# Fifteen halo tiles of h transposed by DMA from SP in place of TensorE: a hybrid attention and pooling layer on eight cores

## The chip, the cores and the metric

The kernel runs as one program on the 8 cores of one Trainium2 chip. Each core computes 1,024 of the 8,192 tokens (batch 2, sequence 4,096) and nothing is exchanged between cores: what a core needs of earlier tokens it computes again from its own copy of x. The metric is the device time in microseconds (us) of the slowest core.

Engines by their names in the profile: PE (TensorE matmul) and PEld (its weight load), DVE (VectorE), ACT (ScalarE), POOL (GpSimd), SP (SyncE). SPq, ACTq and POOLq are the same engines issuing DMAs.

## The reference

```python
for _layer in range(DEPTH):                       # DEPTH = 1, x is (2, 4096, 2048)
    h = rms_norm(x, norm_gain)
    proj = jnp.einsum('bsd,de->bse', h, w_in)     # 16384 columns: q, k, v, z_attn, u_pool, z_pool, gates
    ...
    # --- mixer A: 3 groups (window, dilation) = (128,1), (512,4), (2048,16), 8 heads of 128 each
    q = rms_norm(q.reshape(shp), q_norm_gain)
    k = rms_norm(k.reshape(shp), k_norm_gain)
    for g, (window, dilation) in enumerate(DILATED_GROUPS):
        o_g, lse_g = dilated_window_attention(partial_rope(q[:, :, g], pos), partial_rope(k[:, :, g], pos),
                                              v[:, :, g], window, dilation)
    ...
    y_attn = jnp.einsum('bsc,cd->bsd', attn * jax.nn.silu(z_attn), w_branch_attn)
    # --- mixer B: mean over the last 2, 4, 8, 16 tokens minus the token, a 256x256 map per group
    y_pool = jnp.einsum('bsc,cd->bsd', pool * jax.nn.silu(z_pool), w_branch_pool)
    merged = g_attn * y_attn + g_pool * y_pool
    x = x + jnp.einsum('bsd,de->bse', merged, w_out)
```

A query attends to keys up to 2,048 tokens back. A core therefore needs h of its own 1,024 tokens and of the 2,048 tokens ahead of them, the halo, of which k and v are taken.

## The kernel before, in words

**Stages.** (1) The norm and transpose of 24 tiles of x (128 tokens by 2,048 channels each), and beside it the pooling branch: the projections u (`u_block`, `u_group`) and z (`zp_block`, `z_early`) with the pooling and its maps (`u_pool`, `pool_map`). (2) Twelve rounds of attention: `proj_v` for two heads, then `proj_qk` and `attention` for each. (3) Gates, merge and the output projection.

**The tiles of x.** `tiles` orders them: own tiles 0 to 8 as j = 0 to 8 (tile 8 holds 16 own tokens and 112 of the halo), then the halo tiles 14, 13, 12, 0, 1, ..., 11 as j = 9 to 23. For each, `x_task(j)` makes this sequence: ACT squares the tile of x with a sum (L538, writes `xn` as scratch) and takes Ln and Exp of the sum (L462); DVE multiplies (L473) and writes the normed tile `xn`; SP issues the load of tile j+3 into the buffer of `xt` that is now read; PE transposes `xn` in 16 blocks of 128x128 into two banks `p_pnd` (L557), 8 blocks each; ACT (first half of a halo tile, L466) and DVE (second half, L574) copy these to `hTh` (halo) or `hTo` (own), the transposed h that all projections read. `xt` has 3 buffers, `xn` has 2, so that the square of tile j writes the buffer that tile j-2 used. The halo tiles' parts carry `heavy=XLATE`: they are taken up only while the planner sees ACT and DVE less than 4 us behind PE.

**What sets the order.** `Sched.op` appends each instruction to the list of its engine and derives its waits from the buffers that it reads and writes; it also keeps planned times, with a cost for each instruction. `Tasks.pump` and `need_tiles` put pieces of the live tasks between the projection's matmuls by those planned times. Each engine then runs its list in order. A DMA's planned cost is 0.1 us on its engine, and its end comes from `kb` over 540 KB per us and 2.2 us of latency; the real one plays no part in the order.

**The hand-over to stage 2.** The tensors of stage 2 (`vSb`, `vSc`, `kS`, `qS`, `E`, `ND`, `rot`) lie in the memory of `xt`, `xn`, `gb`, `ua`, `ub` and `pt`. `inherit(b, p1)` makes the first write to each of them wait for every user of all of those. The first such write is ACT's copy of `proj_v` from a `p_pp` bank to `vSb` (L466). `p_pp` has 3 banks.

**SP's list in stage 1** holds the loads of x (L513) and the spills `pt_spill<-s_pt` of the pooling branch (L682), which are read back in stage 3. In stage 2 it holds the small copies `s_rot<-s_kS` and `s_rot<-s_qS` within SBUF (L848, L850; 16 partitions each). Weights are loaded from POOL (L481).

Of the kernel before, what the change touches and what calls it, by code (L numbers as in the profile page):

```python
# [11 lines left out]
KC = 16  # L12
# [292 lines left out]
def build_program(debug=False):  # L305
# [16 lines left out]
    with es:  # L322
# [4 lines left out]
        def place(name, shape, dt, at=None):  # L327
            n = 1
            for s in shape[1:]:
                n *= s  # L330
            nbytes = n * (4 if dt == F32 else 2)
            if at is None:
                at = pos[0]
                pos[0] += ((nbytes + 31) // 32) * 32
                assert pos[0] <= limit, (name, pos[0], limit)
            assert at + nbytes <= limit, (name, at, nbytes, limit)
            return nc.alloc_sbuf_tensor_at("s_" + name, shape, dt, offset=at)
# [18 lines left out]
        hTh = place("hTh", [128, KC, THALO], BF16)  # L356
# [21 lines left out]
        xn_t = [zA.put(f"xn{i}", [128, D], BF16) for i in range(2)]  # L378
# [40 lines left out]
        def psb(name):  # L419
# [5 lines left out]
        pnd_t = [psb(f"pnd{i}") for i in range(2)]  # L425

        semnames = (["pe", "act", "dve", "pool", "sp"] + [f"dw{i}" for i in range(NW)]
                    + [f"dx{i}" for i in range(4)] + [f"dc{i}" for i in range(8)] + [f"dp{i}" for i in range(3)]
                    + [f"drot{i}" for i in range(4)] + [f"dwo{i}" for i in range(4)]
                    + [f"dr{i}" for i in range(4)] + [f"do{i}" for i in range(4)])  # L430
        sems = {k: es.enter_context(nc.semaphore("s_" + k)) for k in semnames}
        S = Sched(nc, sems)
# [3 lines left out]
        B_hH = [Buf(f"hH{i}") for i in range(16)]  # L436
# [28 lines left out]
        def acopy(out, in_, n, reads, writes):  # L465
            S.op("act", lambda a: a.copy(out=out, in_=in_), reads=reads, writes=writes, cost=0.17 + n * 0.00083)  # L466
# [30 lines left out]
        xn = Ring(xn_t, "xn")  # L497
# [3 lines left out]
        def issue_x(j):  # L501
            wh, ti = tiles[j]
            i = xt.take("x")
            loaded[j] = i
            if wh == "o" and ti == 8:
                inherit(B_x8, [xt.B[i]])
                S.op("sp", lambda s: s.dma_start(out=xt_t[i][0:16, :], in_=xh[NTOK - 16:NTOK, :]),
                     writes=[xt.B[i]], dsem=f"dx{i}", kb=128)
                S.op("sp", lambda s: s.dma_start(out=xt_t[i][16:128, :], in_=xh[THALO - 128:THALO - 16, :]),
                     writes=[B_x8], dsem="dx3", kb=896)  # L510
                return
            row = ti * 128 if wh == "h" else THALO - PRE + ti * 128
            S.op("sp", lambda s: s.dma_start(out=xt_t[i][:], in_=xh[row:row + 128, :]),  # L513
                 writes=[xt.B[i]], dsem=f"dx{i}", kb=1024)
# [12 lines left out]
        def x_task(j):  # L527
            wh, ti = tiles[j]
            own = wh == "o"
            x8 = [B_x8] if own and ti == 8 else []  # L530

            def gen(me):
                yield Cond(after=[tile_front[j - 1]] if j else [])
                xi = loaded[j]
                c0 = 3 * j
                yield Cond(reads=[xt.B[xi]] + x8, rings=[xn], heavy=0.0 if own else XLATE)
                ni = xn.take(me)
                S.op("act", lambda a: a.activation(out=xn_t[ni][:], in_=xt_t[xi][:], func=AF.Square,  # L538
                                                   accum_out=stat[:, c0:c0 + 1]),
                     reads=[xt.B[xi], B_stat0] + x8, writes=[xn.B[ni], B_st[j]], cost=2.1)  # L540
                act(stat[:, c0 + 1:c0 + 2], stat[:, c0:c0 + 1], AF.Ln, 1, [B_st[j]], [B_st[j]], bias=float(D * EPS))
                act(stat[:, c0 + 2:c0 + 3], stat[:, c0 + 1:c0 + 2], AF.Exp, 1, [B_st[j]], [B_st[j]], scale=-0.5,
                    bias=float(0.5 * np.log(D)))
                stt(xn_t[ni][:], xt_t[xi][:], stat[:, c0 + 2:c0 + 3], gb[:], ALU.mult, ALU.mult, 2048,
                    [xt.B[xi], B_st[j], B_gb] + x8, [xn.B[ni]], cost=2.35)
                xt.free(xi)
                tile_front[j].done = True
                if j + 3 < 24:
                    if x8:
                        inherit(xt.B[xi], x8)  # L550
                    issue_x(j + 3)
                for half in range(2):
                    yield Cond(reads=[xn.B[ni], B_id], rings=[pnd], heavy=0.0 if own else XLATE)
                    pi = pnd.take(me)
                    for k8 in range(8):
                        kc = half * 8 + k8
                        S.op("pe", lambda t, kc=kc, k8=k8, pi=pi: t.transpose(  # L557
                            tp_t[pi][:, k8 * 128:(k8 + 1) * 128], xn_t[ni][:, kc * 128:(kc + 1) * 128], ident[:]),
                            reads=[xn.B[ni], B_id], writes=[pnd.B[pi]], cost=0.056)
                    ks = slice(half * 8, half * 8 + 8)  # L560
                    i_ap = tp_t[pi].rearrange("p (k c) -> p k c", c=128)
                    if not own:
                        parts = [(hTh[:, ks, ti * 128:ti * 128 + 128], i_ap, 1024, B_hH[ti])]
                    elif ti < 8:
                        parts = [(hTo[:, ks, ti * 128:ti * 128 + 128], i_ap, 1024, B_hO[ti])]
                    else:
                        parts = [(hTo[:, ks, TOWN:TOWN + PRE], i_ap[:, :, 0:16], 128, B_hO[8]),
                                 (hTh[:, ks, THALO - 128:THALO - 16], i_ap[:, :, 16:128], 896, B_hH[15])]
                    on_act = half == 0 and (not own or ti % 2 == 1)
                    for (o_ap, p_ap, n, bd) in parts:  # L570
                        if on_act:
                            acopy(o_ap, p_ap, n, [pnd.B[pi]], [bd])
                        else:
                            S.op("dve", lambda v, o_ap=o_ap, p_ap=p_ap: v.tensor_copy(out=o_ap, in_=p_ap),  # L574
                                 reads=[pnd.B[pi]], writes=[bd], cost=0.1 + n * 0.00058)
                    pnd.free(pi)
                xn.free(ni)
                if own and ti == 0:
                    acopy(hTh[:, :, THALO - PRE:THALO], hTo[:, :, 0:PRE], 256, [B_hO[0]], [B_hH[15]])
            return gen  # L580
# [154 lines left out]
        for j in range(9):  # L735
# [6 lines left out]
            if j == 5 or j == 6:  # L742
                z_early(j - 5, w01[2 + j - 5], 0)
        S.op("pool", lambda g: g.dma_start(out=pm[:], in_=pmaps.rearrange("p (g e) -> p g e", g=8)),
             writes=[B_pm], dsem="dc3", kb=1024)
# [373 lines left out]
        for b in [B_pT, B_wo[1]] + tga.B + tgp.B:  # L1119
            inherit(b, B_hH)  # L1120
        S.op("sp", lambda s: s.dma_start(out=pT[:], in_=pt_d.rearrange("p (e t) -> p e t", e=8)),
             reads=[B_ptd], writes=[B_pT], dsem="dp1", kb=2048)
        S.op("dve", lambda v: v.tensor_scalar_mul(out=halfb[:], in0=cst[:, C_BG:C_BG + 32], scalar1=0.5),
             reads=[B_cst], writes=[B_halfb])
# [62 lines left out]
        for cg in range(4):  # L1187
            cs = slice(512 * cg, 512 * cg + 512)
            for tt_ in range(8):
# [4 lines left out]
                    out=xr_t[xi][:], in_=xh[THALO + 128 * tt_:THALO + 128 * tt_ + 128, cs]),  # L1194
                    writes=[xr.B[xi]], dsem=f"dr{xi}", kb=256)
                P, BP = banks[n_out % 4]
                n_out += 1
                for db in range(KC):
# [5 lines left out]
                     reads=[ob.B[oi]], dsem=f"do{oi}", kb=256)  # L1204
# [90 lines left out]
```

How the kernel before makes its waits and increments, by code:

```python
        def run(ename, eng):  # L144
            w = waited[ename]
            for o in streams[ename]:
                for k, d in o.deps.items():
                    if d.eng == "pe" and ename == "pe" and not d.isdma:
                        continue
                    if w[k] < d.semval:
                        eng.wait_ge(sems[k], d.semval)
                        w[k] = d.semval
                ins = o.fn(eng)
                if o.signal:
                    ins.then_inc(sems[o.key], 16 if o.isdma else 1)
            for k, v in final.items():
                if w[k] < v:
                    eng.wait_ge(sems[k], v)
                    w[k] = v
```

## Time and profile before

| | us |
|---|---|
| median of 3 runs | 1662.37 |
| lowest and highest of the 3 | 1601.19 and 1837.11 |
| the profiled execution | 1614.29 |
| its span (core 5, the slowest; the others 1588.8 to 1611.1) | 1612.7 |
| PE busy in it | 1561.1 (97%) |
| DVE, ACT, POOL busy | 635.7, 607.3, 86.9 |
| stage 1 to the first copy to `vSb` | 0 to 224.8 |

The span runs from the first to the last instruction of a core; 1.6 us of the profiled execution lie around it. A busy share is an average over all stages; what a change of stage 1 is worth has to be read in stage 1.

### The profile page before, as it was taken

The page shows a single profiled execution, that of the slowest core. Times are in us where ns is not written, and L with a number is a line of the kernel's source. Part 1 is how long each engine was busy: PE and PEld are TensorE (multiplying, and loading weights), DVE is VectorE, ACT ScalarE, POOL GpSimd, SP SyncE. Part 2 cuts the span into 40 slices and gives each one's busy share as a digit, 9 for nine tenths or more (in the row PEclk, how much of TensorE's full clock was granted, in tenths as well). Part 3 has the DMA queues.
Part 4 walks back from the last instruction along what each step waited for, and adds up shares of the span by engine and source line. Part 5 has one row for each costly group of instructions (what it writes and reads, how often), then busy time and mean ns, then how long its engine had stood idle before and what let it go on. Part 6 is the DMA issues. An engine that isn't in the chain of part 4 may idle for free.

```text
span 1612.7 us, 26994 instructions; the slowest of 8 cores (1588.8 to 1612.7 us)
## 1 busy us (share of the span) xinstructions
PE 1561.1 (97%) x10192; PEld 939.6 (58%) x10192; DVE 635.7 (39%) x830; ACT 607.3 (38%) x988; POOL 86.9 (5%) x168
## 2 busy tenths in 40 slices
PE   4699999999999999999999999999999999999998
PEld 4455575946694567667847784757444444444443
DVE  4676714136433636445056523535531111112221
ACT  4655525344434544545354434553641111111000
POOL 0000000000000000000000000000001100000000
PEclk9988879999999999999999999999999999999999
DMA  8997334031403233333113222133535566542895
GB/s 240 228 229 170 86 59 85 4 58 35 84 3 66 52 53 56 67 58 57 27 34 67 54 40 47 34 71 59 126 70 85 104 105 104 92 72 47 181 215 126
DMA packets 43071, 139.08 MB, mean 86 GB/s; under 512 B 7040, under 2 KB 8064, under 8 KB 39552
## 3 DMA queue, kind: packets, MB, share of 16 engines
q0 software_dynamic: 23552, 85.58, 31.4%
q1 hardware_dynamic: 14640, 43.33, 8.7%
q10 hardware_dynamic: 4752, 8.44, 2.6%
q8 instruction: 83, 1.36, 0.3%
q14 instruction: 44, 0.36, 0.1%
HBM read 207.90 MB, written 10.49 MB: 135 GB/s over the span
## 4 chain that ended last, share of the span: by engine, by line
PE 93%; DMA 2%; ACT 2%; DVE 1%; issue 1%; ACTq 0%; DVEq 0%; SPq 0%; POOLq 0%
PE p_pp L458 77%; PE p_pnd L458 6%; PE p_psc L458 5%; PE p_pS L458 4%; PE p_pnd L557 1%; DMA s_xt<-xh 1%; ACT s_xn L538 1%; DMA pt_spill<-s_pt 1%; DMA s_wr<-w_in 1%; DVE s_xn L473 1%; ACT s_rr L462 1%; DVE s_rr L469 0%; ACT s_stat L462 0%; ACT L538 0%; DVE s_hTo L574 0%
## 5 line engine op out<-in xcount | busy, mean ns | idle before, releaser
L458 PE MATMUL p_pp<-s_hTo,s_wr 128*128 128x512 bf16 (+4 forms) x3616 | 781.2, 371 | 14.6 <-DVE s_hTo L574 6.8
L458 PEld LDWEIGHTS p_pp<-s_hTo,s_wr 128*128 128x128 bf16 x3616 | 347.5, 100 | 384.1 <-issue 47.9
L473 DVE SCALAR_TENSOR_TENSOR s_kS<-p_pp,s_cst,s_rr 128x512 bf16<-128x512 f32 (+1 forms) x96 | 94.7, 986 | 282.2 <-ACT s_rr L462 279.2
L458 PE MATMUL p_pp<-s_wr,s_hTo 128*128 128x256 bf16 x1536 | 178.7, 276 | 0.0
L458 PEld LDWEIGHTS p_pp<-s_wr,s_hTo 128*128 128x128 bf16 x1536 | 161.6, 119 | 8.9
L458 PE MATMUL p_pp<-s_wr,s_hTh 128*128 128x256 bf16 x1344 | 162.0, 275 | 2.3 <-ACT s_vSb L466 2.3
L458 PE MATMUL p_pp<-s_hTh,s_wr 128*128 128x512 bf16 (+1 forms) x768 | 155.3, 353 | 0.0
L462 ACT ACTIVATE s_rr<-p_pS 128x512 f32<-128x512 f32 x144 | 83.6, 581 | 181.2 <-PE p_pS L458 175.2
L458 PEld LDWEIGHTS p_pp<-s_wr,s_hTh 128*128 128x128 bf16 x1344 | 145.9, 137 | 6.3 <-issue 2.9
L462 ACT ACTIVATE s_rr<-s_rr 128x512 f32<-128x512 f32 x208 | 128.6, 618 | 19.2 <-ACT s_rr L462 0.4
L481 POOL DMA_DIRECT2D s_wr<-w_in x128 | 67.6, 529 | 1265.9 <-PE p_pp L458 806.3
L458 PEld LDWEIGHTS p_pp<-s_hTh,s_wr 128*128 128x128 bf16 x768 | 70.5, 98 | 75.5 <-issue 0.6
L462 ACT ACTIVATE s_sq<-p_pp 128x512 bf16<-128x512 f32 x144 | 83.1, 577 | 55.3 <-PE p_pp L458 55.2
L473 DVE SCALAR_TENSOR_TENSOR s_tga<-s_tga,p_psc 128x512 f32<-128x512 f32 x32 | 22.0, 687 | 206.6 <-PE p_psc L458 206.6
L462 ACT ACTIVATE s_tga<-p_pp,s_halfb 128x512 f32<-128x512 f32 x32 | 22.0, 687 | 166.7 <-PE p_pp L458 166.6
L458 PE MATMUL p_pp<-s_wo,s_mT 128*128 128x512 bf16 x384 | 84.2, 379 | 0.0
L462 ACT ACTIVATE s_E<-p_psc 128x512 bf16<-128x512 f32 x96 | 57.5, 599 | 59.2 <-PE p_psc L458 58.4
L473 DVE SCALAR_TENSOR_TENSOR s_xn<-s_xt,s_stat,s_gb 128x2048 bf16<-128x2048 f32 x24 | 56.4, 2351 | 45.2 <-ACT s_stat L462 44.7
L473 DVE SCALAR_TENSOR_TENSOR s_qS<-p_pp,s_cst,s_rr 128x512 bf16<-128x512 f32 x48 | 48.5, 1011 | 61.9 <-ACT s_rr L462 58.1
L469 DVE TENSOR_TENSOR s_E<-s_E,s_mskb 128x512 bf16<-128x512 bf16 x96 | 40.8, 425 | 76.2 <-ACT s_E L462 76.0
L466 ACT CAST s_vSc<-p_pp 128x512 bf16<-128x512 f32 (+1 forms) x58 | 33.8, 583 | 96.8 <-PE p_pp L458 96.8
L458 PEld LDWEIGHTS p_pp<-s_wo,s_mT 128*128 128x128 bf16 x384 | 37.6, 98 | 45.3
(70 smaller groups left out, 1198.4 us busy)
## 6 DMA issues: line engine op xcount, KB each, us to landing
s_wr<-w_in POOLq DMA_DIRECT2D x128, 512.0 KB, 6.3
s_xt<-xh SPq DMA_DIRECT2D x23, 1024.0 KB, 9.8
s_wr<-w_y POOLq DMA_DIRECT2D x16, 512.0 KB, 5.9
s_wo<-w_out POOLq DMA_DIRECT2D x16, 512.0 KB, 8.7
s_xr<-xh ACTq DMA_DIRECT2D x32, 256.0 KB, 7.6
out<-s_ob SPq DMA_DIRECT2D x32, 256.0 KB, 6.9
pt_spill<-s_pt SPq DMA_DIRECT2D x8, 256.0 KB, 6.2
s_pT<-pt_spill SPq DMA_DIRECT2D x1, 2048.0 KB, 14.3
```

Of the source, the lines that this page charges most:

```text
L458: S.op("pe", lambda t: t.matmul(out, lhsT=lhsT, rhs=rhs, start=start, stop=stop), reads=reads, writes=writes, cost=n / 2400.0 + 0.0025)
L462: S.op("act", lambda a: a.activation(out=out, in_=in_, func=func, **kw), reads=reads, writes=writes, cost=0.18 + n * 0.00085)
L466: S.op("act", lambda a: a.copy(out=out, in_=in_), reads=reads, writes=writes, cost=0.17 + n * 0.00083)
L469: S.op("dve", lambda v: v.tensor_tensor(out=out, in0=in0, in1=in1, op=op), reads=reads, writes=writes, cost=cost if cost is not None else ...
L473: S.op("dve", lambda v: v.scalar_tensor_tensor(out=out, in0=in0, scalar=scalar, in1=in1, op0=op0, op1=op1), reads=reads, writes=writes, co ...
L481: S.op("pool", lambda g: g.dma_start(out=wr[:, i], in_=src[row0:row0 + 128, :].rearrange("p (k c) -> p k c", k=KC)), behind=behind, writes ...
L538: S.op("act", lambda a: a.activation(out=xn_t[ni][:], in_=xt_t[xi][:], func=AF.Square, accum_out=stat[:, c0:c0 + 1]), reads=[xt.B[xi], B_s ...
L557: S.op("pe", lambda t, kc=kc, k8=k8, pi=pi: t.transpose(tp_t[pi][:, k8 * 128:(k8 + 1) * 128], xn_t[ni][:, kc * 128:(kc + 1) * 128], ident[:]),
```

## The change

For the 15 halo tiles (j = 9 to 23) `x_task` no longer goes on to PE. After the normed tile and the load of tile j+3, SP issues 16 DMA transposes, each of a 128x128 block of bf16 (32 KB) from `xn` in SBUF to `hTh` in SBUF. They count on a semaphore of the `xn` buffer, `dt0` or `dt1`. The own tiles keep the old way.

```diff
-                    + [f"dx{i}" for i in range(4)] + [f"dc{i}" for i in range(8)] + [f"dp{i}" for i in range(3)]
+                    + [f"dx{i}" for i in range(4)] + ["dt0", "dt1"] + [f"dc{i}" for i in range(8)] + [f"dp{i}" for i in range(3)]
...
                 if j + 3 < 24:
                     if x8:
                         inherit(xt.B[xi], x8)
                     issue_x(j + 3)
+                if not own:
+                    for kc in range(KC):
+                        S.op("sp", lambda s, kc=kc: s.dma_start_transpose(
+                            out=hTh[:, kc, ti * 128:ti * 128 + 128], in_=xn_t[ni][:, kc * 128:kc * 128 + 128]),
+                            reads=[xn.B[ni]], writes=[B_hH[ti]] if kc == KC - 1 else [], dsem=f"dt{ni}", kb=32)
+                    xn.free(ni)
+                    return
                 for half in range(2):
                     yield Cond(reads=[xn.B[ni], B_id], rings=[pnd], heavy=0.0 if own else XLATE)
```

With the change the program holds 240 transposes fewer on PE, 15 copies fewer on ACT and 15 fewer on DVE, and 240 DMAs more on SP; the line numbers below the diff are 7 higher than before. In the rows that follow `s_xt_61` to `_63` are the three buffers of x, `s_xn_64` and `_65` the two of the normed tile (semaphores `s_dt0` and `s_dt1`).

SP's list before, around the first halo tiles:

```order
L513 DMA s_xt_61<-xh 128x2048 [waits s_dx0,s_act,s_dve]
L513 DMA s_xt_62<-xh 128x2048 [waits s_dx1,s_act,s_dve]
L513 DMA s_xt_63<-xh 128x2048 [waits s_dx2,s_act,s_dve]
L513 DMA s_xt_61<-xh 128x2048 [waits s_dx0,s_act,s_dve]
L682 DMA pt_spill<-s_pt_72 128x1024 [waits s_dve]
L513 DMA s_xt_62<-xh 128x2048 [waits s_dx1,s_act,s_dve]
```

The same place with the change, from the load of tile 12:

```order
L513 DMA s_xt_61<-xh 128x2048 [waits s_dx0,s_act,s_dve]
L554 DMA_TRANSPOSE s_hTh<-s_xn_65 128x128 x16
L513 DMA s_xt_62<-xh 128x2048 [waits s_dx1,s_act,s_dve]
L554 DMA_TRANSPOSE s_hTh<-s_xn_64 128x128 x16
L513 DMA s_xt_63<-xh 128x2048 [waits s_dx2,s_act,s_dve]
L554 DMA_TRANSPOSE s_hTh<-s_xn_65 128x128 x16
L689 DMA pt_spill<-s_pt_72 128x1024 [waits s_dve]
L513 DMA s_xt_61<-xh 128x2048 [waits s_dx0,s_act,s_dve]
```

The 16 transposes of a tile stand behind the load of the tile three later, and every later load and spill stands behind them. The end of SP's stage 1 list with the change, and the first entry of stage 2:

```order
L554 DMA_TRANSPOSE s_hTh<-s_xn_64 128x128 x15
L689 DMA pt_spill<-s_pt_72 128x1024 [waits s_dve,s_dp0]
L554 DMA_TRANSPOSE s_hTh<-s_xn_65 128x128 [waits s_dve]
L554 DMA_TRANSPOSE s_hTh<-s_xn_65 128x128 x15
L689 DMA pt_spill<-s_pt_73 128x1024 [waits s_dve,s_dp0]
L855 DMA s_rot_86<-s_kS_82 16x768 [waits s_dve,s_dx0,s_act,s_dx1,s_dx2,s_dt0,s_dt1,s_dc1,s_dp0]
```

The last spill of stage 1 stands behind all 240 transposes, where before it stood behind other spills only. On ACT, the difference around the squares of tiles 11 and 12 (L538), with what each waits for:

```order
-L466 COPY s_hTh<-p_pnd 128x8x128 [waits s_pe]
-L538 ACTIVATE s_xn_65,s_stat<-s_xt_63 128x2048 [waits s_dx2,s_dve,s_pe]
-L462 ACTIVATE s_stat<-s_stat 128x1 [waits s_act] x2
 L466 COPY s_ua_67<-p_pp 128x144 [waits s_pe]
 L466 COPY s_ua_68<-p_pp 128x144 [waits s_pe]
 L462 ACTIVATE s_rr_59<-p_pp 128x512 [waits s_pe]
 L462 ACTIVATE s_rr_59<-s_rr_59 128x512 [waits s_act] x2
+L538 ACTIVATE s_xn_65,s_stat<-s_xt_63 128x2048 [waits s_dx2,s_dve,s_dt1]
+L462 ACTIVATE s_stat<-s_stat 128x1 [waits s_act] x2
+L462 ACTIVATE s_rr_60<-p_pp 128x512 [waits s_pe,s_dve]
+L462 ACTIVATE s_rr_60<-s_rr_60 128x512 [waits s_act] x2
```

The square of tile 11 waited for PE's transposes of tile 9; now it waits for tile 9's sixteenth DMA (`s_dt1`), and the silu and `ua` copies of the pooling branch stand behind it.

## Rows read from the trace of the kernel before

**Rows 1.** The page: busy time, and the chain that ended last, by engine
```profile
PE 1561.1 (97%) x10192; PEld 939.6 (58%) x10192; DVE 635.7 (39%) x830; ACT 607.3 (38%) x988; POOL 86.9 (5%) x168
PE 93%; DMA 2%; ACT 2%; DVE 1%; issue 1%; ACTq 0%; DVEq 0%; SPq 0%; POOLq 0%
```

**Rows 2.** Windows of core 5: length, busy us of PE, PEld, DVE, ACT, POOL (count), PEclk, DMA, GB/s
```profile
80.00:120.00 40.00, 37.98 (x237) 21.98 (x236) 29.29 (x34) 23.16 (x37) 2.11 (x4) 0.81 1.02 228
120.00:160.00 40.00, 39.09 (x229) 21.86 (x228) 27.19 (x27) 21.55 (x38) 2.11 (x4) 0.81 0.71 172
160.00:200.00 40.00, 39.09 (x217) 21.24 (x216) 29.67 (x29) 22.02 (x38) 1.58 (x3) 0.81 0.40 91
```

**Rows 3.** PE, timeline: start us, length us, operation; one halo tile's 16 transposes
```profile
105.09 1.23 PE L557 MATMUL p_pnd<-s_ident,s_xn 128*128 128x128 bf16 x16
106.14 9.29 PE L458 MATMUL p_pp<-s_hTo,s_wr 128*128 128x346 bf16 x36
```

**Rows 4.** Groups of instructions, 68 to 212 us: busy us, mean ns, idle before
```profile
L557 PE MATMUL p_pnd<-s_ident,s_xn 128*128 128x128 bf16 x240 | 19.7, 242 | 0.0
L466 ACT COPY s_hTh<-p_pnd 128x1024 bf16<-128x1024 bf16 x15 | 15.2, 1012 | 26.1 <-PE p_pnd L557 26.1
L574 DVE COPY s_hTh<-p_pnd 128x1024 bf16<-128x1024 bf16 x15 | 10.3, 686 | 9.9 <-ACT s_hTh L466 9.6 <-PE p_pnd L557 0.2
```

**Rows 5.** DVE, timeline: the normed tiles j = 9 and j = 23
```profile
65.81 2.35 DVE L473 SCALAR_TENSOR_TENSOR s_xn<-s_xt,s_stat,s_gb 128x2048 bf16<-128x2048 f32 x1 [5.78 <-ACT s_stat L462]
...
182.43 2.35 DVE L473 SCALAR_TENSOR_TENSOR s_xn<-s_xt,s_stat,s_gb 128x2048 bf16<-128x2048 f32 x1 [0.24 <-ACT s_stat L462]
```

**Rows 6.** ACT, timeline: the square of tile 11, and the first copies of stage 2
```profile
73.02 1.91 ACT L538 ACTIVATE s_xn<-s_xt 128x2048 bf16<-128x2048 f32 x1
...
224.81 1.93 ACT L466 CAST s_vSb<-p_pp 128x512 bf16<-128x512 f32 x3 [12.51 <-DMA pt_spill<-s_pt]
```

**Rows 7.** PE, timeline: the first and last of three bank fills, and the fourth
```profile
210.45 2.27 PE L458 MATMUL p_pp<-s_wr,s_hTh 128*128 128x256 bf16 x16
...
218.85 4.38 PE L458 MATMUL p_pp<-s_wr,s_hTo 128*128 128x256 bf16 x32
225.54 3.21 PE L458 MATMUL p_pp<-s_wr,s_hTh 128*128 128x256 bf16 x16 [2.31 <-ACT s_vSb L466]
```

**Rows 8.** SP, timeline: a spill's issue, and the first and fourth of four copies
```profile
93.92 0.33 SPq L682 DMA_DIRECT2D pt_spill<-s_pt  x1
...
255.75 0.60 SPq L848 DMA_DIRECT2D s_rot<-s_kS  x1
...
257.62 0.57 SPq L850 DMA_DIRECT2D s_rot<-s_kS  x1
```

**Rows 9.** DMA issues of the span: KB each, median us from issue to landing
```profile
s_rot<-s_qS SPq DMA_DIRECT2D x48, 32.0 KB, 2.0
s_rot<-s_kS SPq DMA_DIRECT2D x48, 32.0 KB, 1.9
```

**Rows 10.** DMA issues, 120 to 160 us: KB each, median us to landing
```profile
s_xt<-xh SPq DMA_DIRECT2D x4, 1024.0 KB, 8.8
pt_spill<-s_pt SPq DMA_DIRECT2D x2, 256.0 KB, 5.3
```

**Rows 11.** PE, timeline: groups of 128x128 matmuls in the first 40 us
```profile
24.75 1.91 PE L458 MATMUL p_pp<-s_hTo,s_wr 128*128 128x128 bf16 x16
...
32.06 3.37 PE L458 MATMUL p_pp<-s_hTo,s_wr 128*128 128x128 bf16 x32
35.26 1.06 PE L557 MATMUL p_pnd<-s_ident,s_xn 128*128 128x128 bf16 x16
36.16 1.95 PE L458 MATMUL p_pp<-s_hTo,s_wr 128*128 128x128 bf16 x32
```

**Rows 12.** DMA queue of SP, 700 to 1100 us: packets, MB, share of 16 engines
```profile
q1 hardware_dynamic: 2112, 1.92, 1.8%
```

## The prediction

> **What bounds the kernel now.** I read the page first: PE is busy for 97% of the span, and 93% of the chain that ended last is PE [rows 1]. So a change that takes work off PE can win that work, and one that makes PE wait loses the wait in full. Then the windows of stage 1, where all that changes lies: from 80 to 200 us PE is busy for 38 to 39 of each 40 us, DVE for 27 to 30, ACT for 22 to 23, and the DMA engines fall from full (1.02) over 0.71 to 0.40 [rows 2]. TensorE's granted clock is 0.81 there on this core, between the two levels of 1.2 and 2.4 GHz in the mean, and the times below are taken as they stand at it. ACT and DVE are not the bound, but both run in order, so what counts for them is not their busy time but what stands in front of PE's evacuations. Last the hand-over: the first copy to `vSb` begins at 224.81, after 12.51 us in which ACT waited for the landing of the last spill, and PE, which had filled its three banks since 210.45, lost only 2.31 us to it [rows 6, 7]. That landing is where every user of stage 1's memory has to be done. The profile has 1614.3 us, 48 us (3%) under the median of the three runs shown and 13 above the lowest; I sum against 1614.3.
>
> **What is removed.** PE's 16 transposes of a halo tile begin at 105.09 and the next matmul at 106.14, 1.05 us later [rows 3]. 15 tiles make 15 x 1.05 = 15.7 us of PE, all of it on the bound. (The group's 19.7 us of busy time [rows 4] counts overlapping pipelines, so I take the difference of starts.) The 15 copies on ACT (15.2 us) and 15 on DVE (10.3 us) [rows 4] lie beside PE's work and are worth nothing by themselves. So the change can win at most 15.7 us, 1.0%: 1598.6 us. A gain over 2% is not in the rows at all, unless some knock-on of equal size comes with it.
>
> **What is added: one chain on SP.** 240 transfers of 32 KB, on one queue, in order. The normed tile j = 9 is ready at 65.81 + 2.35 = 68.2 us [rows 5], the earliest start. If one transfer takes t us of the queue, the 240 take 240 t. Between and behind them SP also issues 11 loads of x and 8 spills at 0.33 each [rows 8], 6 us, and the last spill stands behind all 240 and must land, 5.3 us [rows 10], before ACT may write `vSb`. First copy of stage 2: 68.2 + 240 t + 6 + 5.3 = 79.5 + 240 t, against 224.8. The chain has no pauses once t is over some 0.4: the square of tile j+2 waits for the transfers of tile j, but meanwhile those of j+1 run for 16 t, and square, sums and multiply of a tile take only about 5 us (from 1.91 on ACT and 2.35 on DVE [rows 5, 6]).
>
> While it runs, ACT is the engine that waits: the square of tile 11 ran at 73.02 [rows 6] and now needs tile 9's sixteen landed, 68.2 + 16 t. Behind it on ACT are the `ua` copies and silus of the pooling branch; with them not done PE's three `p_pp` banks stay full. So PE loses in pieces throughout stage 1 what the chain is late. These pieces are not added to the end of the chain, they are its early part. The 15.7 us of PE saved fall into those waits and are worth nothing if the chain is the bound.
>
> Delay of stage 2: D = 79.5 + 240 t - 224.8 = 240 t - 145.3. It is zero at t = 0.61, and 2% of the time (32 us, about what a measurement of this kernel can tell from no change) at t = 0.74. Under 0.6 the chain is hidden and PE's saving shows.
>
> **What t is.** No row shows a transposing transfer. The nearest: SP copies of the same 32 KB, SBUF to SBUF. Four in a row are issued at 255.75 to 257.62, one every 0.62 us [rows 8]; each lands 1.9 to 2.0 us after its issue [rows 9], so copies overlap. If transposes pipeline like them, t = 0.62; if each has to be through before the next moves, t = 2.0. A lower bound from the engines: SP's queue had 2112 packets in 1.8% of 16 x 400 us, 0.055 us each [rows 12]; a 128x128 block has 128 rows of 256 B where the copy has 16 of 2 KB, so 8 packets per engine, 0.44 us, if pieces stay whole rows, and more if the turned side has smaller ones. The issue alone could be as short as the spill's 0.33 [rows 8]. Ends: 0.33 (hidden, 1598.6 us) and 2.0. I take the middle of the two rows of the same size, (0.62 + 2.0) / 2 = 1.3: a block with eight times the rows of the copy, and its sides crossed, is unlikely to pass as smoothly as the copy, and nothing says that none overlap. This is the choice on which the forecast stands.
>
> The Trainium skill, "VectorE: DVE Perf Modes", section "The three transpose paths", gives 1309 ns for the DMA crossbar transpose of 128x128 bf16 and 390 ns for TensorE's, and its rules say to use TensorE where a PSUM destination will do: a rule against this change. An estimate by that page: 240 x 1.309 = 314 us of queue, D = +169 us. TensorE's price there is not this trace's, where one costs 1.05 / 16 = 0.066 us in a row of sixteen [rows 3]; for the DMA's no row here speaks.
>
> **The sum.** 240 x 1.3 = 312; first copy at 391.5; D = +167. At the restart PE has been idle for long: in the first 40 us, after such gaps, 16 matmuls of 128x128 took 1.91 us and 32 took 3.37, later 1.06 and 1.95 [rows 11], the pace of 1.2 and then of 2.4 GHz. PE's dense work went at half pace from 24.75 to 35.26, so I add 4 us once. 1614.3 + 167 + 4 = 1785 us. Nothing gives it back: stage 2 is PE-bound and begins with all of h ready. Its own range, t from 0.74 to 2.0, is 1647 to 1953 (2.0: D = +335, and 4).
>
> **Rivals.**
> *Hidden (ends not slower).* The transfers pipeline like the copies. At t = 0.62 the first `vSb` copy is at 79.5 + 148.8 = 228.3, 3.5 us late: 1618 us. At 0.5 it would be at 199.5, before PE is ready for it, and the time is 1598.6. It decides at t = 0.61. For it: four copies issued within 2 us, engines free to 0.3 and 0.6 after 120 us [rows 2], a floor of 0.44 by packets. Against it: it needs the transposing form to cost no more than the cheapest reading of a copy. The Trainium skill, "Advanced Engine Details and Errata", section "X-Bar Transpose (TRN2)", says that transpose DMAs are as fast as regular ones; by that rule this rival is the result. No row here bears it out or denies it.
> *The queue's engines are the limit.* If t is time of the DMA engines and not of issue, the 11 loads of x between the transfers take their full 8.8 us in the same queue [rows 10] in place of 0.33, 93 us more: 1785 + 93 = 1878. For it: the DMA engines were full until 120 us [rows 2]. Against: loads and transfers may overlap, and the loads of the other queue too.
> *It doesn't do what it says.* If the transfer were broken into single 2-byte elements, 16,384 over 16 engines at 0.055 would be 56 us each and 13 ms in all. The built program has 240 transposing instructions with whole blocks, so I give it almost nothing.
>
> **How the numbers follow.** The chain bounds, t between 0.74 and 2.0: 0.52, at 1785. Engines the limit: 0.12. Over 2.0 or broken up: 0.02. Hidden, from -16 to +32 us: 0.32. Faster by over 2%, which needs twice what is removed: 0.02. So slower 0.66, same 0.32, faster 0.02. The range takes in the hidden case and t = 2.0: 1590 to 1955. Against the median of runs, which lies 3% over the profile, the forecast would read 1838, inside the range.
>
> **What would show it.** In the changed profile: DMA_TRANSPOSE on SPq with its start distance, which is t; the first `vSb` copy at 79.5 + 240 t, released by a DMA; ACT's squares (L538) waiting for the DMAs into `hTh` from tile 11 on; PE waiting for ACT from about 90 us, with stage 1's PE share far under 97% and the stages behind as before. If SP's starts are 0.5 us apart and ACT's squares don't wait, the rival stands. What would make the forecast wrong: t near 0.6, or squares that stall so that the chain has gaps and ends later than 240 t.

## The result, and the profile after

The changed kernel takes 1799.59 us in the median of its runs, against 1632.14 for the kernel before in the same comparison: the ratio is 1.123, with a 95% interval of 1.1213 to 1.1248. The ratio leaves out the executions in which one die ran at a lower clock, which the medians hold. The profiled execution took 1795.7 us, its slowest core 1794.0. The forecast was 1785.

The page of the kernel after: busy time, the queue of SP, and the chain that ended last by engine.

```profile
PE 1557.4 (87%) x9952; PEld 927.8 (52%) x9952; DVE 625.2 (35%) x815; ACT 592.9 (33%) x973; POOL 86.9 (5%) x168
...
q1 hardware_dynamic: 53040, 51.23, 10.3%
...
PE 76%; SPq 18%; DMA 2%; ACT 1%; issue 1%; DVE 1%; ACTq 0%; DVEq 0%
```

Of [rows 1], PE's busy time has hardly moved (1561.1 before), but its share of the chain went from 93% to 76%, and SPq, which had none, has 18% (its transposes at L554 alone 17%, by the page's list of lines). An engine that only issues has become the bound of a stage. The queue's share says the opposite of its issuer: q1 moved 38,400 packets more than before (14,640 and 8.7% then), for 10.3% x 1794.0 - 8.7% x 1612.7 = 44.5 us of all 16 engines. That gives an estimate of 0.185 us for a transpose; it is a net figure, since the loads of x in the same queue also landed sooner (7.0 us in place of 9.8). The transfers are cheap for the DMA engines and dear for SP.

The same kernel, the transposes as a group on SP: duration on the queue in ns (minimum, median, maximum), first and last start, who waited, and issue to landing.

```profile
L554 SPq DMA_TRANSPOSE s_hTh<-s_xn x240: 1084/1203/2857, 68.7 to 398.7; - x120
...
  ACT s_xn L538: 207.6, 13
...
DMA to landing us min/median/max: 2.2/2.9/15.3
```

SP's timeline, start and length in us, at the first two halo tiles and at the end of stage 1 (compare [rows 8]: a load or a spill keeps SP 0.33):

```profile
68.34 0.33 SPq L513 DMA_DIRECT2D s_xt<-xh  x1
68.72 24.01 SPq L554 DMA_TRANSPOSE s_hTh<-s_xn  x16
92.95 0.39 SPq L513 DMA_DIRECT2D s_xt<-xh  x1
93.40 22.25 SPq L554 DMA_TRANSPOSE s_hTh<-s_xn  x16
...
314.23 65.17 SPq L554 DMA_TRANSPOSE s_hTh<-s_xn  x48
379.56 0.45 SPq L689 DMA_DIRECT2D pt_spill<-s_pt  x1
380.11 19.76 SPq L554 DMA_TRANSPOSE s_hTh<-s_xn  x16
400.04 0.45 SPq L689 DMA_DIRECT2D pt_spill<-s_pt  x1
```

From 68.72 to 399.87 SP has one chain with hardly a pause (the longest stop, 2.0 us, is before a spill): 317.7 us in transposes, so 1.32 us each in the mean, and 13.5 us of loads, spills and steps between. The first tile, with the DMA engines full (share 0.98 from 60 to 100 us), took 24.0 us and its transposes a median of 10.0 to land; most of the later ones took 20 to 22 us, with a share of 0.47 from 120 to 360 us. The first copy of stage 2 on ACT, and what PE did then, answer to [rows 6, 7]:

```profile
402.64 1.93 ACT L466 CAST s_vSb<-p_pp 128x512 bf16<-128x512 f32 x3 [31.35 <-DMA pt_spill<-s_pt]
```

```profile
403.37 3.58 PE L458 MATMUL p_pp<-s_wr,s_hTh 128*128 128x256 bf16 x16 [22.67 <-ACT s_vSb L466]
...
410.51 1.91 PE L458 MATMUL p_pp<-s_wr,s_hTh 128*128 128x256 bf16 x16
```

The last spill's landing releases ACT, and ACT releases PE. The bracket on the ACT line names the spill, but the spill itself took 2.6 us; what made it late is the 240 instructions ahead of it on SP, which only SP's timeline shows.

Waits of ACT and of PE from 0 to 450 us: total, times, longest.

```profile
ACT s_xn L538 <- DMA s_hTh<-s_xn: 207.6, 13, 24.2
ACT s_vSb L466 <- DMA pt_spill<-s_pt: 31.3, 1, 31.3
```

```profile
PE p_pp L458 <- ACT s_ua L466: 70.7, 6, 14.6
PE p_pp L458 <- ACT s_rr L462: 46.2, 3, 19.7
PE p_pp L458 <- DVE s_rr L469: 27.1, 3, 18.3
...
PE p_pp L458 <- ACT s_vSb L466: 22.7, 1, 22.7
```

Among all eleven kinds of wait that PE has in this window, none is for a halo transfer. PE waits for copies and silus that stand behind a square on ACT, and the square (L538) is what waits for the transfers. Windows, in the columns of [rows 2]:

```profile
120.00:160.00 40.00, 20.17 (x84) 9.25 (x84) 13.75 (x14) 4.12 (x9) 1.05 (x2) 0.76 0.43 98
180.00:220.00 40.00, 13.91 (x64) 7.61 (x64) 7.50 (x6) 9.14 (x16) 0.53 (x1) 0.67 0.40 97
...
480.00:1790.00 1310.00, 1301.18 (x8317) 766.84 (x8315) 475.82 (x661) 453.14 (x731) 70.70 (x134) 1.00 0.39 72
```

In the two windows of stage 1 PE is busy for a half and a third of the time, and where it idles most its granted clock is 0.67, between the two levels of 1.2 and 2.4 GHz in the mean, so its busy microseconds also do less. Behind stage 1 nothing has changed: 99% busy at full clock.

### The profile page after: what moved, and what is told of

Same layout as the page of the kernel before. It is cut to its first block, busy times and chain, and to the rows that moved or that the text cites. A ratio compares the mean times of both kernels' runs of the same rounds, so it can differ in the third digit from the quotient of the medians.

```text
span 1794.0 us, 26683 instructions; the slowest of 8 cores (1784.3 to 1794.0 us)
## 1 busy us (share of the span) xinstructions
PE 1557.4 (87%) x9952; PEld 927.8 (52%) x9952; DVE 625.2 (35%) x815; ACT 592.9 (33%) x973; POOL 86.9 (5%) x168
## 3 DMA queue, kind: packets, MB, share of 16 engines
q1 hardware_dynamic: 53040, 51.23, 10.3%
## 4 chain that ended last, share of the span: by engine, by line
PE 76%; SPq 18%; DMA 2%; ACT 1%; issue 1%; DVE 1%; ACTq 0%; DVEq 0%
PE p_pp L458 62%; SPq L554 17%; PE p_pnd L458 5%; PE p_psc L458 4%; PE p_pS L458 3%; DMA s_xt<-xh 1%; ACT s_xn L538 1%; DVE s_xn L473 1%; DMA s_rot<-s_qS 0%; PE p_pnd L564 0%; DMA s_rot<-s_kS 0%; DMA pt_spill<-s_pt 0%; SPq L513 0%; ACT s_rr L462 0%; DVE s_kS L469 0%
## 5 line engine op out<-in xcount | busy, mean ns | idle before, releaser
L458 PEld LDWEIGHTS p_pp<-s_hTo,s_wr 128*128 128x128 bf16 x3616 | 351.3, 101 | 527.1 <-issue 165.3
L538 ACT ACTIVATE s_xn<-s_xt 128x2048 bf16<-128x2048 f32 x24 | 45.8, 1910 | 211.4 <-DMA s_hTh<-s_xn 207.6
L473 DVE SCALAR_TENSOR_TENSOR s_tga<-s_tga,p_psc 128x512 f32<-128x512 f32 x32 | 22.0, 687 | 207.1 <-PE p_psc L458 207.1
```

The costliest lines, as they stand in the source:

```text
L458: S.op("pe", lambda t: t.matmul(out, lhsT=lhsT, rhs=rhs, start=start, stop=stop), reads=reads, writes=writes, cost=n / 2400.0 + 0.0025)
L473: S.op("dve", lambda v: v.scalar_tensor_tensor(out=out, in0=in0, scalar=scalar, in1=in1, op0=op0, op1=op1), reads=reads, writes=writes, co ...
```

## The experiments

The theories. **A**: SP pays a fixed price for each transposing instruction, whatever its size. **B**: the price is the transfer's, its bytes or rows through the DMA engines. Then: what would be left if SP's price were gone, and what the 15.7 us of PE are worth. In the diffs the changed kernel's line stands with a minus, and three dots stand for lines left out.

**1. A tile in one instruction.** The destination is three-dimensional, the sixteen blocks go out at once: 15 instructions in place of 240.

```diff
-                    for kc in range(KC):
-                        S.op("sp", lambda s, kc=kc: s.dma_start_transpose(
-                            out=hTh[:, kc, ti * 128:ti * 128 + 128], in_=xn_t[ni][:, kc * 128:kc * 128 + 128]),
-                            ...
+                    S.op("sp", lambda s: s.dma_start_transpose(
+                        out=hTh[:, :, ti * 128:ti * 128 + 128], in_=xn_t[ni][:]),
+                        ...
```

> The 16 transposes of a tile are one instruction over the same 512 KB-free block (128x2048 in, 128x16x128 out), the output stays the reference's; 15 transposing DMAs in place of 240. In the changed kernel one instruction keeps SP for 1.2 us (median) whatever the DMA engines do, whose share is 0.45. Theory A (a fixed price for each instruction on SP): SP is kept 1.2 to 2 us per tile, 18 to 30 us in all, the chain is hidden, ACT's squares don't wait, the first vSb copy is at 210 to 225 and the time is before's less up to 15.7 us: ratio to before 0.985 to 1.00. Theory B (the price goes with the blocks or bytes, on SP or in the queue): about 16 x 1.2 = 19 to 20 us per tile, first vSb copy at 385 to 403, ratio 1.11 to 1.125.

Measured: 1.0322 [1.0299, 1.0345]. The group on SP:

```profile
L553 SPq DMA_TRANSPOSE s_hTh<-s_xn x15: 1865/7224/27276, 65.7 to 248.8; - x15
...
  ACT s_xn L538: 84.4, 8
...
DMA to landing us min/median/max: 4.4/15.8/31.5
```

Sixteen blocks can leave SP in 1.87 us, where sixteen instructions took 19 to 24. Most of the loss is gone, so it went with the number of instructions on SP. But the result is in neither forecast: a tile now took a median of 15.8 us to land, and held SP for a median of 7.2. The windows of core 0 (the DMA share is the last number but one):

```profile
60.00:100.00 40.00, 27.95 (x197) 18.01 (x198) 21.35 (x25) 17.28 (x33) 3.16 (x6) 0.88 0.99 250
100.00:140.00 40.00, 26.59 (x117) 12.47 (x118) 20.96 (x22) 15.04 (x26) 1.58 (x3) 0.80 1.17 169
140.00:180.00 40.00, 31.38 (x155) 15.85 (x155) 18.60 (x18) 13.19 (x24) 2.11 (x4) 0.88 1.16 180
```

The share adds up the times of the packets, so packets that overlap can bring it over 1. The engines are full for 120 us, and from 100 to 140 us they move less: 169 GB/s at a share of 1.17, where the same core had 230 at 0.91 in the kernel before. (From 140 to 180 us they move more than before, 180 against 145.) On the slowest core the squares waited 84.4 us for the transfers.

**2. Two instructions for a block**, 64 rows each: 480 instructions for the same bytes.

```diff
-                        S.op("sp", lambda s, kc=kc: s.dma_start_transpose(
-                            out=hTh[:, kc, ti * 128:ti * 128 + 128], in_=xn_t[ni][:, kc * 128:kc * 128 + 128]),
-                            ...
+                        for hr in range(2):
+                            S.op("sp", lambda s, kc=kc, hr=hr: s.dma_start_transpose(
+                                out=hTh[:, kc, ti * 128 + hr * 64:ti * 128 + hr * 64 + 64],
+                                in_=xn_t[ni][hr * 64:hr * 64 + 64, kc * 128:kc * 128 + 128]),
+                                ...
```

> Each 128x128 transpose is issued as two of 64 rows by 128 columns; 480 instructions of half the bytes, the output stays the reference's. Theory A (fixed price): 480 x 1.2 to 1.3 = 576 to 635 us of chain, first vSb copy at 660 to 720, time 2050 to 2110 us. Theory B (price by bytes): as the changed kernel, first vSb copy near 403, 1790 to 1810 us. A mixture a + b x blocks shows in the median of the instruction: 1.2 us again for A, 0.6 us for B.

Measured: 2093.94 us, one execution; the first copy to `vSb` is at 701.78.

```profile
L555 SPq DMA_TRANSPOSE s_hTh<-s_xn x480: 1088/1228/2564, 68.2 to 698.2; - x160
```

Half a block costs SP 1228 ns, a whole one 1203. Against the profiled execution of the changed kernel, 240 instructions more made 2093.94 - 1795.7 = 298 us more, 1.24 us each. Theory A holds for a block and for half of one.

**3. Plain copies** in the transposes' place (the halo's h is not transposed).

```diff
-                        S.op("sp", lambda s, kc=kc: s.dma_start_transpose(
+                        S.op("sp", lambda s, kc=kc: s.dma_start(
```

> The 240 transposes become 240 plain DMA copies of the same 128x128 blocks, same place on SP, same waits; h of the halo then stands untransposed, so that its part of the output is not the reference's. Theory A or B with the transposing form as the cause: a copy keeps SP for 0.33 to 0.6 us, 80 to 145 us in all, the first vSb copy is at 200 to 228 and the ratio to before 0.99 to 1.005. Rival C (240 DMAs on one queue among 1 MB loads are the cause, whatever their form): starts 1.2 us apart or more again, first vSb copy over 380, ratio 1.11 or more.

Measured: 1.0375 [1.0311, 1.044], between the two forecasts.

```profile
L554 SPq DMA_DIRECT2D s_hTh<-s_xn x240: 464/586/6628, 67.3 to 258.4; - x120
...
  ACT s_xn L538: 67.0, 10
```

A copy costs SP half of what a transpose does, near the 0.6 of [rows 8]. Yet 240 of them took 172.2 us of SP (0.72 in the mean, up to 6.6 for one at 79.91, where the DMA share was 1.03), the chain ran from 67.33 to 259.0, and the first copy to `vSb` began at 261.39. "Hidden at the price of a copy" is refuted by the copy.

**4. Half of the tiles.** Only odd j go by DMA, the other seven by TensorE.

```diff
-                if not own:
+                if not own and j % 2 == 1:
```

> Only the halo tiles with odd j (8 of 15) go by DMA, the 7 others by PE as before; the output stays the reference's. All eight lie in the same one of the two xn buffers, so that the square, sums and multiply of the next (5.5 us) can't run under the transfers. Theory of the chain with t = 1.32: 68.2 + 8 x 21.2 + 7 x 5.5 + 5 = 281 for the first vSb copy, 56 us late, ratio 1.03 to 1.04. If only the count matters (240 t - 145 with 128 in place of 240): 68.2 + 170 + 11 = 249, 24 us late, ratio 1.015. If the loss were in PE's starved work and not in the chain (half of the changed kernel's 185): ratio 1.06.

Measured: 1.0578 [1.0562, 1.0594], with the first copy to `vSb` at 299.97 where the chain gave 281. The ratio is close to the 1.06 expected if the loss were in PE's starved work. But the hand-over is later by 299.97 - 200.29 = 99.7 us than on the same core of the kernel before, and the profiled execution, 1689.60 us, is 92.1 over the median before: the lateness of the hand-over covers the whole loss, so the chain stands and its gaps were put too small. SP was in transposes for 171.2 us, but the chain lasted from 66.27 to 297.6: loads, spills and pauses take 60 us. All eight tiles use the same one of the two `xn` buffers, so each has to land before the next can be squared and normed into it, and SP stands still meanwhile. Seven squares waited 99.1 us. Taking back 7 of the 15 tiles brings back about half of the loss.

**5. A third buffer of `xn`**, taken from memory that `pt` gave up, so that squares run one tile further ahead.

```diff
-        xn_t = [zA.put(f"xn{i}", [128, D], BF16) for i in range(2)]
+        xn_t = [zA.put(f"xn{i}", [128, D], BF16) for i in range(3)]
...
```

> The changed kernel with a third xn buffer (pt0 moves into sq's memory and pt1 into that of tab, neither used in stage 1), so that ACT's square of tile j waits for the transposes of j-3. Chain theory: SP's 240 instructions of 1.2 to 1.35 us are the bound, so ACT's waits for s_xn move elsewhere but the first vSb copy stays at 390 to 403 and the time within 1% of the changed kernel's 1800 (1782 to 1815). Rival (the loss is made by the squares at the head of ACT's queue, each waiting for a landing): the first vSb copy comes 15 us or more earlier, under 385, and the time is under 1780.

Measured: 1791.45 us, one execution; first `vSb` copy at 399.54 on the slowest core, squares still 202.1 us behind the transfers. Both lie where the chain had them (1782 to 1815, 390 to 403), and the rival (under 1780, under 385) is out. Where SP never pauses, a buffer more changes when the waits fall, not their sum.

**6. Experiment 1 with the third buffer.**

> One transposing DMA per tile (15 in all) and a third xn buffer. With two buffers that took 1.032 of before: SP is free, ACT waited 84 us in 8 squares for landings of 4 to 31 us, and the DMA engines were full from 60 to 240 us. If the waits of the squares are what costs, a buffer more takes most of them away: ratio 0.99 to 1.01. If the DMA engines are the bound (6 us of all 16 for a tile beside the loads), they stay full and it gains little: ratio 1.02 to 1.03.

Measured: 1.0236 [1.0159, 1.0314]; the interval overlaps that of experiment 1 a little, so a gain by the buffer is likely and not certain. The first `vSb` copies of the eight cores are at 222.3 to 248.7 in place of 229.4 to 261.7; on the slowest core the squares still waited 73.0 us, landing took a median of 11.9 us, and the DMA share was 1.10 to 1.16 from 80 to 200 us. That is what was forecast for engines that stay full. That their load is the cause is argued from the share and the landings: no run took that load away.

**7. One instruction for a tile, for the last eight tiles only**, when the engines have room by [rows 2].

```diff
-                if not own:
+                if not own and j >= 16:
```

> One transposing DMA per tile, only for the tiles j = 16 to 23 (8 of 15), whose normed tiles are made after 120 us, where before's DMA engines were at 0.7 and 0.4. PE is freed of 8 x 1.05 = 8.4 us. If the DMA engines' load is what made one-per-tile slow, these hide better: ratio 0.995 to 1.005. If the squares' waits cost the same per tile (52 us for 15): 28 - 8 = 20 us, ratio 1.012 or more.

Measured: 1.0104 [1.0053, 1.0155], between its two forecasts. The room was not enough: the DMA share was 1.14 from 120 to 160 us, and four squares waited 43.1 us.

**8. A probe ahead of the kernel before**: transposes of 1, 1, 2, 4, 8, 16, 16 blocks and two copies, each waiting for the one before, then transposes beside a weight load and behind an x load. The whole time is not read.

> The kernel before, with a piece ahead of it that times transfers one at a time: transposing DMAs of 1, 1, 2, 4, 8, 16 and 16 blocks of 128x128, two plain copies of a block, then a 16-block transpose beside a 512 KB weight load from POOL, a 16-block and a 1-block one right behind a 1 MB load of x on SP's queue. Fixed price: SP kept 1.1 us for one block and under 2 us for 16; landing 2.2 us for one, 4.4 us for 16. Price by blocks: 1.1 and 17 us. If the load of the engines is what stretched the 16-block transfers to 16 to 31 us, the one beside the weight load lands after 8 us or more and the one behind x after 10 us or more, and SP is kept for several us there; if not, both land within 5 us. Nothing of the time of the whole is read from this run.

Issue to landing, us, on core 4: 1 block 2.31 and 2.24; 2 blocks 2.30; 4 blocks 2.41; 8 blocks 3.08; 16 blocks 4.28 and 4.27; a copy of 32 KB 1.78 and 1.75. SP's timeline in the second part:

```profile
28.40 1.32 SPq L493 DMA_TRANSPOSE s_hTh<-s_xn  x1
37.83 0.38 SPq L510 DMA_DIRECT2D s_xt<-xh  x1
38.26 5.75 SPq L493 DMA_TRANSPOSE s_hTh<-s_xn  x1
46.09 0.48 SPq L498 DMA_DIRECT2D s_hTh<-s_xn  x1
47.85 0.34 SPq L514 DMA_DIRECT2D s_xt<-xh  x1
48.24 1.13 SPq L493 DMA_TRANSPOSE s_hTh<-s_xn  x1
```

With nothing beside it a 16-block transpose held SP for 1.95 and 1.86 us. The first row above (28.40) is the one that a weight load follows 0.5 us later: it held SP for 1.32 (2.00 the second time) but took 7.3 and 8.8 us to land. Right behind a 1 MB x load, 16 blocks held SP for 5.75 (6.57 the second time) and landed after 7.8 and 8.6 us; one block held it for 1.13 and landed after 5.9 and 4.7. So one load beside it about doubles the landing of 4.3 us, less than the 10 us and more forecast behind x. A long transposing instruction behind a load that is still in the DMA engines holds its queue's engine. Experiment 1's median of 7.2 us fits that; its longest, 27.3 us to issue and 31.5 to land, go beyond what one load does here, and no run reproduces them alone.

**9. No transposes at all** for the halo: neither PE nor a DMA makes them (GpSimd writes zeros to the halo's h).

```diff
-                    for kc in range(KC):
-                        S.op("sp", lambda s, kc=kc: s.dma_start_transpose(
-                            ...
+                    S.op("pool", lambda g: g.memset(hTh[:, :, ti * 128:ti * 128 + 128], 0.0),
+                         writes=[B_hH[ti]], cost=0.1)
```

> The 15 halo tiles are neither transposed by PE nor by DMA: POOL, idle otherwise, sets their part of hTh to zero, so that k and v of the halo and what follows from them are not the reference's. This isolates what the removed PE work is worth: by the prediction 15 x 1.05 = 15.7 us at the clock granted to the profiled core of before, 0.066 x 240 x 0.81 = 13 us at the full clock; ratio 0.990 to 0.992, first vSb copy 13 to 16 us earlier. If ACT's and DVE's 25 us of copies were worth something too, under 0.985. If another wait takes its place (the last spill's landing, the weights behind POOL's memsets), 0.995 to 1.0.

Measured: 0.9993 [0.9983, 1.0003]. As the lists stand, taking all of that work off PE, ACT and DVE is worth nothing. In its place are only the zeros on GpSimd, and PE waits for weights, which GpSimd issues, no longer than before (1.8 us against 1.5 on core 2, from 60 to 215 us). The first copies to `vSb` did not come 13 us earlier: they are at 197.6 to 207.1, against 200.3 to 206.5 on six cores of the kernel before. The slowest core, PE, then ACT, then DVE:

```profile
115.89 2.52 PE L458 MATMUL p_pp<-s_hTo,s_wr 128*128 128x347 bf16 x16 [2.17 <-DVE s_rr L469]
132.29 1.32 PE L458 MATMUL p_pp<-s_hTo,s_wr 128*128 128x347 bf16 x4 [13.88 <-DVE s_rr L469]
```

```profile
117.75 1.91 ACT L538 ACTIVATE s_xn<-s_xt 128x2048 bf16<-128x2048 f32 x1 [3.24 <-DMA s_xt<-xh]
...
126.38 1.91 ACT L538 ACTIVATE s_xn<-s_xt 128x2048 bf16<-128x2048 f32 x1 [6.04 <-DMA s_xt<-xh]
```

```profile
129.07 2.35 DVE L473 SCALAR_TENSOR_TENSOR s_xn<-s_xt,s_stat,s_gb 128x2048 bf16<-128x2048 f32 x1 [4.76 <-ACT s_stat L462]
131.35 0.69 DVE L469 TENSOR_TENSOR s_rr<-p_pp,s_rr 128x512 f32<-128x512 f32 x1
```

The squares now come so early that they wait for their x load (15.6 us in four waits; on the same core of the kernel before 3.1 in one), and what stands behind them keeps PE 13.88 us: the square at 126.38 waits for its load, DVE's normed tile at 129.07 for the square's sum, and the `s_rr` product at 131.35, which PE waits for, stands behind the normed tile on DVE.

**10. Four instructions for a tile**, four blocks each.

```diff
-                    for kc in range(KC):
+                    for kc in range(0, KC, 4):
...
```

> Four blocks of 128x128 to an instruction, 60 in all, two xn buffers; the output stays the reference's. From the probe: SP kept 1.1 to 1.3 us and landing 2.4 us alone for 1, 2 or 4 blocks. SP's price is then 4 x 1.3 = 5 us per tile and can't be the bound. If only SP's price and bursts of 16 blocks hurt, the chain is hidden: ratio 0.99 to 1.01. If the DMA engines' load and the landings behind 1 MB loads set it, as with 16 blocks to an instruction (1.032) and with 240 plain copies (1.0375), the ratio is 1.025 to 1.04 again, with ACT waiting 60 to 85 us in its squares.

Measured: 1630.76 and 1636.83 us against a median of 1598.22 before, 1.020 and 1.024. Only these two executions can be compared, so there is no interval; they lie just below the second forecast's 1.025, and the squares waited 58.6 us, just under its 60.

```profile
L554 SPq DMA_TRANSPOSE s_hTh<-s_xn x60: 1191/1585/14867, 68.5 to 244.6; - x60
...
  ACT s_xn L538: 58.6, 8
```

Four blocks leave SP in as little as 1.19 us, the price of one. From 100 to 140 us the DMA share is 1.25. With all 15 tiles and two `xn` buffers, this splitting came out lowest of those tried, by two executions; it does not reach the kernel before.

**11 and 12. Lists planned for a later load.** Experiment 9, and the kernel before, each with the planner's `kb` of an x load raised from 1024 to 2400, so that it plans a square for 6.6 us after the issue and not 4.1. (In the trace a load takes 8.8 [rows 10], so the plan is nearer to it, not equal.)

```diff
-                 writes=[xt.B[i]], dsem=f"dx{i}", kb=1024)
+                 writes=[xt.B[i]], dsem=f"dx{i}", kb=2400)
```

> The kernel before, with the transposes of the 15 halo tiles left out altogether (neither TensorE nor a transfer does them; GpSimd fills the halo's h with zeros, so the kernel leaves that part of the computation out), and the planner's size of an x load raised from 1024 to 2400, so that it plans the squares of a tile for the time at which the loads land in the trace (8.8 us after their issue). Theory A (the 15.7 us of TensorE that go with the transposes came back as waits only because ACT's and VectorE's lists were written for earlier loads): with the lists planned for the real landing, the saving shows, ratio 0.988 to 0.994 to the kernel before, and the squares of ACT wait for x loads under 5 us in all. Theory B (the loads themselves, or other steps of stage 1, are as late as the work that waits for them): 0.997 to 1.003, and the waits stand elsewhere. It is read against the next kernel, which has the same planner's size and keeps the transposes.

> The kernel before with the planner's size of an x load raised from 1024 to 2400 and nothing else: the control of the kernel without transposes that has the same size. The planner only writes its lists in another order. Theory A of that kernel expects this one at 0.997 to 1.005, and the kernel without transposes 10 to 16 us under it; theory B expects both within 4 us of each other.

Measured: 1.0072 [1.0058, 1.0086] without the transposes, 1.0191 [1.0177, 1.0205] with them. Neither theory of these two expectations has the levels right: both kernels are slower than before, so the new order has a cost of its own (on core 2, PE is busy for 23.7 of the 40 us from 60 to 100 in experiment 12, before for 32.1), and why is open. With one planner's setting, the two differ by 1628.6 - 1610.4 = 18.2 us, over theory A's 10 to 16 and far over theory B's 4. On core 2 no square from 60 to 215 us waited for an x load in either. So with lists in which the squares don't wait for loads, the removed work shows at about its size (15.7 us at the clock of 0.81, 13 by experiment 9's estimate at the full one), and some 2 to 5 us more that stay open. That waits for loads are what swallows it in experiment 9 is shown for one stall of 13.88 us; that planning for them wins it back is not shown, since without the transposes the new lists are slower than the old ones (1.0072 against 0.9993).

## Why the prediction was right, and where it was off

**The mechanism.** Right, and shown: one chain on SP, the hand-over behind it. Experiments 1, 2 and 5 tell it from a price by bytes and from a shortage of buffers.

**The price t.** Taken as 1.3 from between two rows of copies, it came out as 1.32. The reasoning for it was not the right one: the range was drawn for how far transfers overlap, and they overlap freely (2.9 us to land, one every 1.2). That the middle of 0.62 and 2.0 fell on the measured value is luck. What counts is what the instruction costs the engine that issues it, and no row of before showed that for a transpose. The figure of the Trainium skill, "VectorE: DVE Perf Modes", section "The three transpose paths", 1309 ns, is near the mean here of the time that one instruction keeps SP (1.32, median 1.20). It is not the time to land, 2.24 to 2.31 us alone, and it goes with the instruction, since 16 blocks in one held SP for 1.86 us alone.

**The sum.** First copy forecast at 391.5, measured at 402.64: start +0.5, 240 t +5.7, loads, spills and steps between +7.5 (6 forecast, 13.5 measured), landing behind the chain 2.8 in place of 5.3, -2.5. That is 11.2, all of the difference. The restart showed in the group of sixteen at 403.37, which took 3.58 us where a later one took 1.91, so it costs some 2 us and not 4. From PE's restart to the end this core has 1390.6 us against 1387.2 before, but that match with the forecast's 4 is chance: from the first copy to `vSb` to the end, the eight cores have 1385.8 to 1391.4 us, before 1387.5 to 1390.0, and the means are the same to 0.1 us. The kernel before restarted too (3.21 us for its group at 225.54).

**What is removed.** "15.7 us of PE, all of it on the bound" was right in size and wrong as a gain: as the lists stand it is worth nothing (experiment 9), and 18.2 us between two kernels with other lists, both slower than before (11 against 12). In this change it fell into waits, as the prediction said it would.

**The rival "hidden".** Its point of decision, t = 0.61, was the step that failed. Copies at 0.72 should have given 79.5 + 240 x 0.72 = 252.3 and a loss of 27.5 us, 1.7%; they lost 3.75%. Two things were missing. The anchor was late: 224.81 is the first copy to `vSb` on the slowest core of that profile and six of its eight cores have it at 200.3 to 206.5 (below, core 2). The granted clock tells them apart: from 140 to 180 us it is 0.81 on cores 4 and 5, as in [rows 2], and 1.00 on the six others (below, core 0), so the same work of PE takes longer on those two.

```profile
206.27 1.93 ACT L466 CAST s_vSb<-p_pp 128x512 bf16<-128x512 f32 x3 [12.80 <-DMA pt_spill<-s_pt]
```

```profile
140.00:180.00 40.00, 38.35 (x257) 22.18 (x255) 32.08 (x35) 23.97 (x41) 2.65 (x5) 1.00 0.57 145
```

With 206.3 the point is t = 0.53, and 252.3 is 46 us late. And the chain has gaps and waits of its own that no t holds, 19.5 us between the copies here (6 in the sum, 13.5 in the changed kernel); they put the first copy to `vSb` at 261.39, 55 us late, and the loss in the profiled execution was 54.6. The rule of the Trainium skill, "Advanced Engine Details and Errata", section "X-Bar Transpose (TRN2)", by which a transpose DMA is as fast as a regular one, is not borne out here for a block of 32 KB: 1203 against 586 ns of SP, 2.24 to 2.31 against 1.75 to 1.78 us to land alone. For larger ones no run compares the two. Even where it held, the rival would have lost: the copies of experiment 3 are regular ones.

**"The engines are the limit".** Not so in this change (share 0.40 to 0.47, x loads landed in a median of 5.5 us from 120 to 210 us). Once SP's price is taken away, experiments 1, 6, 7 and 10 all had windows with a share of 1.14 to 1.25 and ended 1.0% to 3.2% over the kernel before; that the load of the engines is what holds them there is likely, not shown. Experiment 3 lost 3.75% with a share of 0.67 to 0.87 on its slowest core.

**The size of the loss.** The ratio 1.123 is 197 us, more than the 181 between the two profiles, and more than the 171 forecast. The difference is the anchor again: the changed kernel has its first copies at 396.4 to 402.9 on all cores, and 402.64 - 206.37 = 196.3 us on core 3, the slowest of it. The profile of before is of an execution with two late cores; with 206.4 as the anchor the forecast's own chain gives 391.5 - 206.4 = 185. So the term that was too small is the delay D, 167 in place of 196: 18 by the late anchor, 11 by the chain.

## What to carry to other kernels

Price a DMA three ways before moving work to it: what the instruction costs its issuer, how long it takes to land, and what it takes of the DMA engines; here these were 1.3, 2.9 and 0.19 us, and the first decided. Then look at what stands behind it in the issuer's list and behind its waiter in the other engines' lists, for those waits are where the time shows. And read the anchor of a sum (when must it be done?) on every core, not on the slowest alone.

## What was not expected of the hardware

- SP's price of a transposing instruction is nearly independent of size: a median of 1.23 us for 64 rows and 1.20 for 128; at best 1.19 for four blocks and, with nothing beside it, 1.86 to 1.95 for sixteen.
- With large instructions the packets of the same transposes are open for longer: q1 had 13.6% of 1647.4 us in the time of its packets with one instruction for a tile, 10.3% of 1794.0 with sixteen, for the same bytes (51.2 MB). Whether that is the size of the instruction or the shorter time in which all streams meet, the runs don't tell apart. Beside them a 512 KB weight load landed in a median of 15.3 us from 60 to 240 us; in the kernel before (core 2, 60 to 200 us) in 10.1 (core 5: 9.3).
- A busy DMA engine reaches back into the issuer: a transpose of 16 blocks held SP for 1.86 to 1.95 us alone, 5.75 and 6.57 right behind a 1 MB load, and up to 27.28 in experiment 1, with every load behind it.
